# Raw expert-weight chunks loaded five slots ahead of their use, and three scatter-adds to a slot, in the routing stage of a one-core decoder-layer kernel

## What is computed

```python
q = (t @ w_query).reshape(T, PEER_HEADS, 2, PEER_HALF)
s = einsum('thpc,hpkc->thpk', q, sub_keys)
top_s, top_i = lax.top_k(s, PEER_TOPK)
...                                   # 16 x 16 sums of pairs, best 16 of them
experts = take_along_axis(cand_i, best_j); gate = softmax(best_s)
act = gelu(einsum('pd,phkd->phk', xb, expert_down[eb]), approximate=False)
y = einsum('phk,phkd->pd', gb * act, expert_up[eb])
```

## Time and profile before

| | |
|---|---|
| median of 3 runs | 4422.36 us |
| the profiled execution | 4412.74 us, of which the span of its instructions is 4411.0 us |
| TensorE busy | 3978.6 us, 90% of the span |
| VectorE, ScalarE, GpSimd busy | 59%, 31%, 38% of the span |
| mean granted TensorE clock | 0.951 of full |
| first to last down matmul slot | 1959.9 to 3295.8 us of the span |

### The profile page before, as it was taken

How to read it: one execution, slowest core, us unless ns; L and a number is a source line. 1 busy time by engine, 2 the same in 40 slices (tenths; PEclk the granted TensorE clock), 3 DMA queues, 4 the chain that set the end, 5 groups by cost and what they waited for, 6 DMA issues and landing times. The chain is left out here.

```text
span 4411.0 us, 61280 instructions
## 1 busy us (share of the span) xinstructions
PE 3978.6 (90%) x21744; PEld 3588.3 (81%) x21744; DVE 2585.5 (59%) x5114; ACT 1368.0 (31%) x2139; POOL 1693.8 (38%) x1159
## 2 busy tenths in 40 slices
PE   9999994978888888988798999978988999999997
PEld 7888884867887667988797999978986888888885
DVE  2154103545555333136877888655547888888888
ACT  2143212652222211114545546255212222212220
POOL 0000004614444013000638523888434655555556
PEclk9999996989999998999998999999998999999998
DMA  3222226631222432233367785977978888888884
GB/s 129 95 95 101 96 75 166 160 87 44 74 74 83 168 103 81 76 104 111 77 204 214 238 287 186 287 200 211 373 260 310 294 284 289 299 280 292 290 289 186
DMA packets 390922, 801.82 MB, mean 182 GB/s; under 512 B 65264, under 2 KB 204400, under 8 KB 389744
## 3 DMA queue, kind: packets, MB, share of 16 engines
q1 hardware_dynamic: 280176, 531.25, 35.8%
q0 software_dynamic: 110592, 268.62, 19.8%
HBM read 623.40 MB, written 154.32 MB: 176 GB/s over the span
## 5 line engine op out<-in xcount | busy, mean ns | idle before, releaser
L1923 PE MATMUL r_psd<-x1h,r_dh 128*128 128x384 f32 x2048 | 705.8, 345 | 29.5 <-DVE r_dl L1720 26.4
L1923 PE MATMUL r_psd<-x1l,r_dh 128*128 128x384 f32 x2048 | 691.8, 338 | 0.0
L1923 PE MATMUL r_psd<-x1h,r_dl 128*128 128x384 f32 x2048 | 691.4, 338 | 0.0
L2168 PE MATMUL e_psy<-e_uh,e_Ch 128*128 128x512 f32 x1536 | 599.9, 391 | 32.7 <-DVE e_Cl L2093 29.3
L1696 POOL DMA_INDIRECT W<-r_put,r_place x256 | 420.7, 1643 | 484.3 <-DVEq L1870 397.3
L2168 PE MATMUL e_psy<-e_ul,e_Ch 128*128 128x512 f32 x1536 | 599.2, 390 | 0.0
L2168 PE MATMUL e_psy<-e_uh,e_Cl 128*128 128x512 f32 x1536 | 599.0, 390 | 0.0
L1923 PEld LDWEIGHTS r_psd<-x1h,r_dh 128*128 128x128 f32 x2048 | 392.1, 191 | 31.1 <-DVE r_dl L1720 27.7
L1687 POOL DMA_INDIRECT r_rows<-in_down_rows,ids x256 | 259.1, 1012 | 396.9 <-DVE coef L1738 350.1
L2062 POOL TENSOR_TENSOR e_araw<-e_araw,e_W 128x768 f32<-128x768 f32 x128 | 257.9, 2014 | 396.4 <-DMA e_W<-W 395.1
L1738 DVE CUSTOM_DVE_ANT_0 r_rows<-r_rows,r_psx 128x1024 f32<-128x1024 f32 x256 | 304.9, 1216 | 172.7 <-DMA r_rows<-in_down_rows,ids 167.7
(11 more groups left out here) (326 smaller groups left out, 7348.2 us busy)
## 6 DMA issues: line engine op xcount, KB each, us to landing
r_draw<-in_down SPq DMA_DIRECT2D x128, 512.0 KB
e_uraw<-in_up SPq DMA_DIRECT2D x128, 512.0 KB
act<-r_act SPq DMA_DIRECT2D x128, 384.0 KB
e_araw<-act SPq DMA_DIRECT2D x128, 384.0 KB
e_W<-W SPq DMA_DIRECT2D x128, 384.0 KB
W<-r_W SPq DMA_DIRECT2D x32, 1024.0 KB
p_wraw<-in_w_in SPq DMA_DIRECT2D x58, 512.0 KB
hT<-p_out SPq DMA_DIRECT2D x58, 512.0 KB, 2.9
```

Source lines behind the costliest of these rows:

```text
L1923: ins = nc.tensor.matmul(psd[n][:, h, 0:HD], a[c % DEEP][:, k, :], b[:, k, h * HD:(h + 1) * HD], start=(k == 0 and m == 0), stop=(k == KD ...
L2168: ins = nc.tensor.matmul(bank[:], a[s][:, t * P:(t + 1) * P], v[s][:, h * HALF:(h + 1) * HALF], start=(q == 0 and m == 0), stop=(q == G - ...
```

## The change

In SyncE's program the loads of chunks 3 and 4 are taken out ahead of the loop, and slot c then loads chunk c + 5 instead of chunk c + 3. The buffers stay three, so the load of chunk c + 5 waits for `d_lo` of chunk c + 2, where that of chunk c + 3 waited for `d_lo` of chunk c. In GpSimd's program three adds into W stand in a slot in place of four: the 128 adds of tile 1 take the slots 14 to 56 (they took 14 to 45), those of tile 6 the slots 70 to 112 (70 to 101), the last slot of each holding two.

```diff
-    PER_SLOT = 4
+    PER_SLOT = 3
...
-    scatters = {t: range(routed_in[t] + 1, routed_in[t] + 1 + P // PER_SLOT) for t in SCATTERED}
+    scatters = {t: range(routed_in[t] + 1, routed_in[t] + 1 - (-P // PER_SLOT)) for t in SCATTERED}
...
+            for c in range(2):
+                sp.wait_ge(sem("d_lo"), START + c + 1)
+                load_d(c + DEEP)
             for c in range(PK):
-                if c + DEEP < PK:
-                    sp.wait_ge(sem("d_lo"), START + c + 1)
-                    load_d(c + DEEP)
+                if c + 2 + DEEP < PK:
+                    sp.wait_ge(sem("d_lo"), START + c + 3)
+                    load_d(c + 2 + DEEP)
                 sp.wait_ge(sem("gelu"), START + c + 1)
                 sp.dma_start(g.act[c], act_out[c % 2][:]).then_inc(sem(f"st_a{c % 2}"), 16)
...
-                        for e in range(PER_SLOT * (c - span.start), PER_SLOT * (c - span.start + 1)):
+                        for e in range(PER_SLOT * (c - span.start), min(PER_SLOT * (c - span.start + 1), P)):
```

## The result

The changed kernel takes 4379.24 us (median of four runs, 4376.2 to 4384.15), the kernel before beside it 4421.27: a ratio of 0.9909, 95% interval 0.9898 to 0.9921, 42 us faster. I had forecast 4371, range 4338 to 4410. Measured again as the first experiment it gave 0.9915 (0.9899 to 0.9931). The stage itself shrank by 34.5 us in it, and what lies ahead of and behind the stage, which the change doesn't touch, was 6 us longer.

What follows compares the result with a forecast made beforehand. TensorE is busy 90% of the span; in the changed stage it idles for late rows, with GpSimd full in slots 88 to 102. Terms -22 - 23 - 9 - 4 + 7 = -51 us gave 4361.7, plus 9.6 to the median: 4371, range 4338 to 4410.

Steps and rivals of the forecast that it cites:

- Slots 88 to 102: GpSimd, full with adds and gathers, drops under TensorE's 10.1 us a slot with one add less: -22 us.
- Slots 83 to 87: Three adds a slot let GpSimd catch up; of TensorE's 14.9 us wait at slot 87, 7 stay: -23 us.
- nine lists of 8.8 and one of 9.8 bring it to list 85 at 94.6: GpSimd's adds and gathers per slot from slot 75; a row landing 4.55 us after its gather leaves a 1 us wait.
- The DMA bound of 7 us: Slots 75 to 82: the DMA engines need 0.9 us a slot more than GpSimd, 7 us over eight slots.
- Slots 32 to 35: Shorter GpSimd work cuts about 11 of VectorE's 22.5 us of row waits: -9 us, between 0 and -18.
- the added wait of SyncE: SyncE's wait for `d_lo` of chunk c + 2 ahead of slot c's store: 0 for TensorE.
- Slots 57 to 59: Earlier loads remove 6.5 us of VectorE's lag, adds work against it: -4 us, between +6 and -13.7.
- Slots 103 on: Slots 102 to 112: eleven slots get three adds, GpSimd falls behind, DMA engines are full: +7 us, between 0 and +16.
- GpSimd alone: Rival: everything is late for GpSimd alone, rows still land in 4.5 us: -85 us, 4337; chance 0.10.
- Only the steady stretch pays: Rival: slots 88 to 102 and a little from 83 to 86 gain, group starts keep their lag: about -25, 4397; chance 0.17.
- No change: Rival: gains and costs cancel within 9 us, 4422; chance 0.05.
- Slower: Rival: adds move to slots with full DMA engines, 18 us onto TensorE while rows stay late by landing: 4440; chance 0.08.

Runs made afterwards that it cites:

- the repeat: The changed kernel as it is, timed again beside the kernel before: 4386.3 us, 0.9915.
- head in five slots: The changed kernel, but 16 adds fill five slots (4, 3, 3, 3, 3), each add that waits for earlier ones first in its slot: 4368.8 us, 0.9874.
- the same 16 adds in five slots but slots 75 to 82 eased: The changed kernel with adds fitted by slot, two a slot in slots 75 to 82, none in 103 to 110: 4361.7 us, 0.9870.
- six slots a head: The changed kernel, but 16 adds fill six slots (3, 3, 3, 3, 2, 2), every 16th first in its slot: 4358.5 us, 0.9857.

## Why the prediction was right, and which term was not

By its own steps, from the two profiles; the repeat in brackets.

- **Slots 88 to 102**: -22 forecast, -20.3 (-18.6). That adds and gathers on GpSimd set the pace holds. That three adds give the pace back to TensorE does not quite: the list was to be 9.76 us and was 10.4 with its waits, so GpSimd stayed full and 4 us were left, where I had 2. With a head in five slots, which leaves no wait for adds here, they still took 155.3; with the same 16 adds in five slots but slots 75 to 82 eased, 152.1, within 1 us of TensorE's pace. So the lag that GpSimd and VectorE bring along from the slots ahead was missing from the sum as well.
- **Slots 83 to 87**: -23 forecast, -10.3 (-10.8). This is the mis-sized term, and in part it came in another place. I had worked out only the wait at slot 87, which was to fall from 14.9 us to 7 and is 15.8; slots 83 to 86, of whose 12.7 us of loss the working says nothing, gave 11.2. In the repeat slots 83 to 86 gave 8.2 and slot 87 2.6. The step was "nine lists of 8.8 and one of 9.8 bring it to list 85 at 94.6" and the landing 4.55 us later. It counted adds by their mean of the earlier trace rows and left out that one add in 16 waits for all before it. In the kernel before such a wait stood behind gathers and cost 2.6 us in slots 75 to 87; with three adds to a slot it stands behind an add in two cases of three and cost 10.7. With the head in five slots and the waits behind gathers, 4.6 us came back here, 6 in slots 103 to 125, and 17 us of time in all. The DMA bound of 7 us, the other half of the step, is not what held slot 87: without adds the landing is as slow as with them, and only the issue is earlier. What I also had wrong was the 4.55: it was one of the shortest, while rows that VectorE waited for in that same trace took 4.4 to 9.1 us, and up to 8.9 in slots 83 to 87; around slot 85 a row was used 8.2 us after its gather even with the waits hidden, and three adds less in five slots bring 4 to 5 us.
- **Slots 32 to 35**: -9 forecast, -10.3 (-5.2), as sized within the spread of two profiles. Inside it a loss was hidden that I had put at 0, the added wait of SyncE: I looked at the products' store behind it and at ScalarE's Gelu, and not at the W store behind that, which ScalarE waits for at the start of the next group. It costs about 7 us with six slots a head (52.1 against 45.2).
- **Slots 57 to 59**: -4 forecast, -5.4 (-5.3). The loads do it: -7.8 with loads alone. The adds take 2.4 of that back, as foreseen in kind, though alone they gave -2.8, for which no run here gives a reason.
- **Slots 103 on**: +7 forecast, +10.2 (+8.9). Right in place and cause: slots 111 to 115 stretch with VectorE 18 to 20 us behind in slots 110 to 114. It fell to 4.2 with the head in five slots, whose waits are hidden and whose adds end three slots earlier, and to 0 with six slots a head, whose adds end five slots later but stand less dense.
- **The signs.** ScalarE's waits for chunks vanished (0.2 us) and the lag from slot 103 on came from rows, as I had said. Three signs failed: the 15 slots took 155.5 us for "152 to 155", VectorE went on waiting for rows (51.3 us) and GpSimd hardly for dots (1.2), and the first gate slot's wait was 15.8 for "under 8". And both things by which I was to be wrong happened in slots 88 to 102: GpSimd stayed full, and four rows took 8.3 to 8.7 us to land. So the forecast holds as a time and as a direction, and its picture of the new limit does not.
- **The rivals.** "GpSimd alone" (4337) had rows landing in 4.5 us, which they don't, and its time is not reached even without tile 6's adds (4353). It has a chance of 0.10 in the list and 0.09 in the sum of chances, a slip that changes nothing. "Only the steady stretch pays" (4397) fails by the -10 in two other windows and the -5 in a third. "No change" fails by the interval of the ratio. "Slower", decided by a row taking over 8 us in slots 71 to 102, fails: such rows exist, and the time is 42 us less.

The forecast of 4371 lies nearer to 4379 than its terms deserve; that is luck. The sum was -51 where the stage gave -34.5, and the rest of the profiled execution was 6 longer, 22 us of error in all; and the other way I added 9.6 from the profiled execution to the median, where after's profiled execution lay 4.9 above its median, which takes 14.5 of the 22 back. The loads alone bring a sixth of the gain (7 of 42 us), and on top of three adds a slot 2 us that can't be told from none (4386.3 against 4388.6).

## What to carry to other kernels

Before changing how many instructions stand in a slot, list the waits that come every so many instructions and see what will stand directly ahead of each: a wait for one's own DMA costs little behind a few us of other work (at most 3.8 us over all profiles here) and its whole landing directly behind the DMA itself (up to 6.9 us). Where an engine is full in one stretch and idle in another, spread its deferrable work by the slot's own free time, and check the slots where another engine's long pieces meet the start of a new phase. When a load is moved ahead past a wait, read on in that queue until the next group's consumer, not only to the next instruction.

## What the runs showed of the hardware

- An add of 128 four-byte elements, waited for directly behind it, held GpSimd 4.05 to 4.58 us in slots with a DMA share of 0.69, and up to 6.9 elsewhere. In slots 14 to 27, which have no gathers (DMA share 0.44 in the kernel before), the same kind of wait took 1.6 to 2.5 us, and 4.7 and 5.2 in one profile each. Behind gathers it took up to 2.6 in the kernel before, and at most 3.8 in any profile.
- A DMA share of 1.02 in eight slots does not by itself make VectorE wait for rows that are asked for early: without tile 6's adds its waits for rows in slots 75 to 87 come to 6.3 us, though the rows that it waited for in slots 83 to 87 took 8.1 to 10.0 us from gather to dot, but for one of 4.7.
- VectorE's two-input subtraction lengthens one GpSimd instruction in a slot by about half a us in the earlier trace rows (an add) and by 1.2 above (a gather).
- The last W store of tile 0, 1 MB, had landed 10.8 us behind its issue in the changed kernel (2330.39 to 2341.19), and 10.0 to 15.8 us behind it in the ten other profiles where ScalarE waited for it.
